# Turned tiles set between the quarters of the rising products, with attention's beginning and the merge's load order changed too

## The reference

```python
z  = x @ w_in                                   # queries, keys, values, indexer, gates
ya = sparse_attention(...)                      # 8 heads, top-256 keys by an indexer
yb = sliding_window_attention(...)              # 8 heads, window 128, sinks
merged = sigmoid(gA) * (ya @ w_pa) + sigmoid(gB) * (yb @ w_pb)
x1 = layer_norm(alpha * x + merged @ w_o, ln1_g, ln1_b)
u  = x1 @ w_up                                  # 1024 -> 6144
c  = conv_b + sum(shift(u, j) * conv_w[j] for j in range(3))   # causal, per channel
x2 = layer_norm(alpha * x1 + (gelu(c[:, :3072]) * c[:, 3072:]) @ w_down, ln2_g, ln2_b)
```

## Time and profile before

| | us |
|---|---|
| median of 3 runs | 3387.13 (3385.55 to 3394.36) |
| the profiled execution | 3393.38, of which the span 3391.6 |
| PE busy | 3236.4 (95%) |
| DVE busy | 2445.2 (72%) |
| ACT busy | 1673.5 (49%) |
| POOL busy | 1002.5 (30%) |
| mean granted TensorE clock | 0.981 of full speed |

### The profile page before, as it was taken

One profiled execution on the slowest core, in us unless ns is written; L12 is line 12 of the kernel. 1 busy time (PEld: TensorE's weight loads), 2 busy tenths in 40 slices (PEclk: granted clock), 3 DMA queues, 4 the chain that ended last, 5 costly groups with the idle time before them and its releaser, 6 DMA issues.

```text
span 3391.6 us, 40080 instructions
## 1 busy us (share of the span) xinstructions
PE 3236.4 (95%) x14200; PEld 2568.6 (76%) x14248; DVE 2445.2 (72%) x3632; ACT 1673.5 (49%) x2290; POOL 1002.5 (30%) x592
## 2 busy tenths in 40 slices
PE   7999999996899999989998999999999999999998
PEld 5788878874566666667887788887788888888887
DVE  5899999966666666446665799999888888343344
ACT  5669898215566676663222344444544444311211
POOL 1012232324566666650021134442233331000000
PEclk9999999997999999999999999999999999999999
DMA  6423333453232221035565332233222223533522
GB/s 173 60 75 100 97 109 100 130 167 97 74 84 64 59 65 49 7 111 194 177 248 174 113 104 102 100 122 132 97 91 75 94 87 133 193 109 112 174 98 95
DMA packets 219185, 376.78 MB, mean 111 GB/s; under 512 B 30573, under 2 KB 119933, under 8 KB 211182
## 3 DMA queue, kind: packets, MB, share of 16 engines
q1 hardware_dynamic: 217934, 369.86, 34.6%
q0 software_dynamic: 1056, 4.36, 0.3%
HBM read 276.24 MB, written 97.80 MB: 110 GB/s over the span
## 4 chain that ended last, share of the span: by engine, by line
PE 62%; DVE 6%; ACT 3%; issue 3%; DMA 2%; POOL 1%; SPq 1%; POOLq 0%; DVEq 0%; ACTq 0%
PE rs_ps L88 16%; PE rs_ps L89 15%; PE rs_ps L90 15%; PE rs_ps L2016 2%; PE rs_ps L2043 2%; PE rs_ps L2017 2%; PE rs_ps L1972 2%; PE rs_ps L2045 2%; PE rs_ps L2044 2%; PE rs_ps L2019 1%; PE rs_ps L2021 1%; PE rs_ps L2022 1%; DMA m_xp<-x 1%; DMA m_pr<-in_w_pb_dram 1%; DVE m_sg L1618 1%
## 5 line engine op out<-in xcount | busy, mean ns | idle before, releaser
L88 PE MATMUL rs_ps<-m_xh,m_uh 128*128 128x512 f32 x1344 | 526.8, 392 | 0.2 <-DVE m_ul L1666 0.2
L90 PE MATMUL rs_ps<-m_xh,m_ul 128*128 128x512 f32 x1344 | 524.8, 390 | 0.0
L89 PE MATMUL rs_ps<-m_xl,m_uh 128*128 128x512 f32 x1344 | 524.7, 390 | 0.0
L1160 POOL TENSOR_TENSOR plo<-pf,phi 128x1024 fp32r<-128x1024 f32 x168 | 401.7, 2393 | 266.5 <-ACT phi L1271 260.8
L88 PE MATMUL frt_acc<-frt_xh,frt_wh 128*128 128x512 f32 x864 | 338.8, 392 | 8.8 <-issue 4.5
L89 PE MATMUL frt_acc<-frt_xl,frt_wh 128*128 128x512 f32 x864 | 338.0, 391 | 0.0
L90 PE MATMUL frt_acc<-frt_xh,frt_wl 128*128 128x512 f32 x864 | 337.7, 391 | 0.0
L88 PE MATMUL rs_ps<-m_wh,m_hh 128*128 128x512 f32 x768 | 299.0, 389 | 1.4 <-DVE m_hl L1725 1.2
L90 PE MATMUL rs_ps<-m_wh,m_hl 128*128 128x512 f32 x768 | 298.8, 389 | 0.0
L89 PE MATMUL rs_ps<-m_wlo,m_hh 128*128 128x512 f32 x768 | 298.8, 389 | 0.0
L88 PEld LDWEIGHTS rs_ps<-m_xh,m_uh 128*128 128x128 f32 x1344 | 253.8, 189 | 52.9 <-DVE m_ul L1666 0.6
(11 more groups left out here) (289 smaller groups left out, 7429.7 us busy)
## 6 DMA issues: line engine op xcount, KB each, us to landing
m_ur<-in_w_up_dram SPq DMA_DIRECT2D x48, 1024.0 KB, 6.1
m_wr<-in_w_down_dram SPq DMA_DIRECT2D x60, 512.0 KB, 4.8
zt<-frt_out SPq DMA_DIRECT2D x108, 256.0 KB, 4.5
frt_wr<-in_w_main_dram SPq DMA_DIRECT2D x51, 512.0 KB, 4.1
ht<-m_cg SPq DMA_DIRECT2D x48, 512.0 KB, 3.4
...
```

The lines of the kernel that those rows point to most:

```text
L88: pe.matmul(out, ahi, bhi, start=first, stop=False)
L89: pe.matmul(out, ahi, blo, start=False, stop=False)
L90: return pe.matmul(out, alo, bhi, start=False, stop=last)
L1160: pool.tensor_tensor(plo[:, k % PS, :], pf[:, k % PS, :], f32(phi[:, k % PS, :]), ALU.subtract).then_inc(S["pl"], 1)
```

## The change

It has four parts.

1. SP's order in the merge: the gates of unit u + 2 are loaded in iteration u, behind the weights of unit u + 3, so each unit's gates go out one iteration later; the residual rows go from m = 2 to 5 to m = 4 to 7; the rows of operands 0 and 1 from m = 3 to m = 5 of the last quarter.
2. Attention's beginning: the first `blo` goes from POOL to DVE, and `round_near(1)` from behind the first exponential to right behind `round_values`.
3. PE at k = 0, 23 and 24: a product can be given an operand to turn, and then one tile follows each of its quarters (three passes). The product's counter is raised ahead of the fourth tile. The wait for all of `rd1` now stands ahead of product 0.
4. ACT's and DVE's orders at k = 23 and 24 follow this. Their order at k = 0 is unchanged.

```diff
@@ load_unit (SP)
+            def load_weights(u):
                 if u >= R:
                     sp.wait_ge(T["ab"], u - R + 1)
                 for a, w in enumerate((w_pa, w_pb)):
-                    sp.dma_start(pr[u % R][:, a], w[m]).then_inc(pld[u % R], 16)
+                    sp.dma_start(pr[u % R][:, a], w[u % KT]).then_inc(pld[u % R], 16)
+
+            def load_gates(u):
+                q, m = u // KT, u % KT
                 if u >= R:
                     sp.wait_ge(T["md"], u - R + 1)
...
                     if u + R < NU:
-                        load_unit(u + R)
+                        load_weights(u + R)
+                    if u and u + R <= NU:
+                        load_gates(u + R - 1)
...
-                    if q and 2 <= m < 2 + TB:
-                        sp.wait_ge(st[m - 2], 16 * q)
-                        load_res(TB * q + m - 2)
+                    if q and m >= TB:
+                        sp.wait_ge(st[m - TB], 16 * q)
+                        load_res(TB * q + m - TB)
...
-                    elif q == 3 and m == 3:
+                    elif q == 3 and m == 5:
                         load_rows(0, 0)
                         load_rows(0, 1)
@@ POOL
-            pool.wait_ge(S["bhd"], 1)
-            pool.tensor_tensor(blo[:, 0], near[:, 0], f32(bhi[:, 0]), ALU.subtract).then_inc(S["bl0"], 1)
@@ ACT
                     round_values()
+                    round_near(1)
...
                     exponential(first[b] + x)
-                    if b == 0:
-                        round_near(1)
@@ DVE, attention and k = 23, 24
             dve.tensor_copy(bq[:, 1, :, P:2 * P], nearq[:, 1, :, 0:P]).then_inc(S["rnd"], 1)
+            dve.wait_ge(S["bhd"], 1)
+            dve.tensor_tensor(blo[:, 0], near[:, 0], f32(bhi[:, 0]), ALU.subtract).then_inc(S["bl0"], 1)
...
-                if r != NS - 1:
-                    conv(r - 1, 0)
-                if r == NS:
-                    low_x(1, 5, 0)
+                conv(r - 1, 0)
                 if r < NK:
                     low(r, 6)
                 if r == NS - 1:
                     low_x(1, 0, 0)
-                    conv(r - 1, 0)
+                elif r == NS:
+                    low_x(1, 5, 0)
@@ PE
+            def turn_tile(p, r, b):
+                i, n = 7 * p + r, TB * (7 * p + r) + b
+                if b == 0:
+                    pe.wait_ge(T[f"rl{i % 2}"], 16 * (i // 2 + 1))
+                if n >= 3:
+                    pe.wait_ge(T["xld"], n - 2)
+                for j in range(4):
+                    last = pe.transpose(ps[:, turn_bank(n), j * P:(j + 1) * P], xw[:, i % 2, b, j * P:(j + 1) * P], ident[:])
+                last.then_inc(T["tr"], 1)
...
-            def product(k, j):
+            def product(k, j, turned=None):
...
-                last.then_inc(T["pm"], 1)
+                    if kk == 3:
+                        last.then_inc(T["pm"], 1)
+                    if turned:
+                        turn_tile(*turned, kk)
...
-            product(0, 0)
-            turn(0, 2, 0)
-            turn(0, 2, 1)
...
+            pe.wait_ge(T["rd1"], NB)
+            for j in range(5):
+                product(0, j, (0, j + 2))
             product(0, 5)
             for k in range(1, NK):
...
+                beside = {NS - 1: {1: (1, 0), 6: (1, 1), 3: (1, 2), 4: (1, 3), 5: (1, 4)}, NS: {0: (1, 5), 2: (1, 6)}}.get(k, {})
```

More of the change, by code:

```diff
@@ L1469, in _ @@
                 if r == NS - 1:
-                    high_x(1, 1, 1)
                     high_x(1, 2, 0)
@@ L1885, in _ @@
                 elif r == NS:
+                    low_x(1, 6, 0)
                     low_x(1, 6, 1)
@@ L1890, in _ @@
                     low_x(1, 2, 1)
-                    low_x(1, 3, 0)
                 if more:
@@ L1896, in _ @@
                 if r == NS - 1:
+                    low_x(1, 3, 0)
                     low_x(1, 3, 1)
[L1898 removed]
                 if more:
@@ L1901, in _ @@
                 if r == NS - 1:
+                    low_x(1, 4, 0)
                     low_x(1, 4, 1)
@@ L2075, in turn @@
                 for b in (2 * half, 2 * half + 1):
-                    n = TB * i + b
-                    if n >= 3:
-                        pe.wait_ge(T["xld"], n - 2)
-                    for j in range(4):
-                        last = pe.transpose(ps[:, turn_bank(n), j * P:(j + 1) * P], xw[:, i % 2, b, j * P:(j + 1) * P], ident[:])
-                    last.then_inc(T["tr"], 1)
+                    turn_tile(p, r, b)
+            def turn_tile(p, r, b):
[7 more added lines that the diff above has]
+                last.then_inc(T["tr"], 1)
             def products(u):
```

30 lines of the change are left out of this document (6 added, 24 removed).

## The result

The changed kernel takes 3409.95 us (median of four runs, 3407.98 to 3411.45) against 3386.34 (3380.3 to 3394.36) for the kernel before: the ratio is 1.0066, with a 95% interval of 1.0048 to 1.0085. It is 22 us slower, where +8 was forecast and 3408 was the upper end of the range. The direction came out. So did the waits worked out for attention, k = 0, and k = 23 and 24, within 2 us each; the merge did not, and the clock took more than was put down for it.

What follows compares the result with a forecast made beforehand. PE, busy for 95% of the span, was taken as the bound. Terms -8.0, -5.0, +9.4 and +3.2 gave -0.4, with the clock +8.0; on the median 3387.13 that made 3395.1 us, range 3374 to 3408.

Steps and rivals of the forecast that it cites:

- Attention, -8.0: Attention's beginning: first exponential 3.4 us earlier, and 4.6 of a 7.39 us DVE wait reaching PE; -8.0 us.
- The merge, -5.0: Merge: gains at the last unit and last quarter, less costs of later gates, sum to -5.0 us.
- The last unit's -6.6: Merge, last quarter: the last unit's stall goes, -4.8 us, and the slow stretch behind it, -1.8.
- The terms for the gates: Merge: later gates cost +1.6 us in the first quarter, +1.2 and +1.4 at second units of quarters 1 and 2.
- -2.6: Merge, last quarter's first stalls: later gates let rows go out some 3 us earlier, 2.6 of it gained.
- a sign of being wrong: Merge, quarter 0: the prediction is wrong if the gates make ACT wait for over 4 us.
- k = 0, +9.4: k = 0: stalls grow from 5.4 to 16.7 us; with 1.9 of slow stretch set aside, +9.4 us.
- k = 23 and 24, +3.2: k = 23 and 24: stalls +5.7 us, single tiles +0.8, slow stretches of 3.3 set aside; +3.2 us.
- The clock: Outside the merge, six stalls over 2.7 us each bring a slow stretch of PE's clock at 1.4 us: +8.4.
- The rival "slow clock": Places that change: eleven of thirteen stalls bring slow stretches at 1.6 us, +17.6 for 8.4, total 3404.3; chance 0.22.
- The third rival: k = 0, 23 and 24: tiles hide their chains, few stalls reach 2 us, total about 3371; chance 0.14.
- The Trainium skill's rule: Attention's beginning: shared SBUF interfaces would let POOL's memset hold DVE's moved two-input subtract, giving 1.7 us less.

Runs made afterwards that it cites:

- e5: The kernel before with only the rows of operands 0 and 1 loaded at m = 5 of the last quarter: 3386.16 us, ratio 0.9991.
- e2: The kernel before with SP's changed load order in the merge alone: 3395.51 us, ratio 1.0026.
- e13: The kernel before with the changed load order but without its later gates: 3385.12 us, ratio 0.9988.
- e6: The kernel before with only the gates loaded one unit later: 3402.08 us, ratio 1.0041.
- e15: The kernel before with only the first blo moved to DVE, round_near(1) left in place: 3385.73 us, ratio 0.9994.
- e7: The kernel before with k = 0's tiles between quarters, the rd1 wait, and ACT's and DVE's orders there made to fit: 3391.55 us, ratio 1.0007.

## Why the prediction was wrong, point by point

- **Attention, -8.0: right in its sum, by luck in its parts.** It measured -8.6 in the mean of the profiles, of which -7.2 are waits of PE and the rest clock. The parts were 3.4 and 4.6 and came out near 2 and 5. The first fell short because the cast ahead of the subtract took 2.37 us for 0.67; the second gave more than I let reach PE. The chain `phi`, `plo` was next, as said, but not as long as allowed for.
- **The merge, -5.0: this is the step that failed.** The last unit's -6.6 held: -6.0 between the mean of six profiles with e5's line and that of seven without. The terms for the gates were too small by far. They stood at +1.6, +1.2 and +1.4, with -2.6 for a gain of theirs in the last quarter, +1.6 in all; by e2 and e13 the gates cost 7.2 us, and in e6, without the other moves, 15. In the first quarter I priced the gates of one unit, where ACT waited for three, 4.6 us in sum, which is over the 4 us that I had named as a sign of being wrong. PE's waits there grew by 4.9 us (by 3.0 in e2) for +1.6. At the second units the wait became 3.10 and 2.75 where I had 2.1 to 2.3, with a slow stretch behind each that I had not counted there. The -2.6 did not come: the two waits of the last quarter fell by 1.05 in sum, and in e2 not at all. The chain that I named, from POOL's last difference to the quarter's first pass, is as said: 21.0 us lie between the starts of the two in the kernel before, the changed one, e2, e5, e13 and e15. The rows also went out earlier, at 1743.57 for a mix begun at 1747.57, before at 1744.91 for 1745.32. But they landed no earlier: POOL's first difference of them began 7.9 us behind the start of the mix, 7.5 before, and ahead of the last group POOL still stood for 7.89 us:

```profile
1782.97 1.29 POOL L1197 TENSOR_TENSOR m_xd<-m_xp 128x512 f32<-128x512 f32 x1 [7.89 <-DMA m_xp<-x]
```

  I had taken an earlier issue for an earlier landing. What held the rows up on the way is not shown.
- **k = 0, +9.4 with the clock apart: right.** Waits of 15.1 us for 16.7, each at its place; e7 shows that they are ACT's and DVE's orders, as argued.
- **k = 23 and 24, +3.2 with the clock apart: right in its waits,** all five within 0.4 us.
- **The clock: under-sized.** I removed 7.0 us of old slow stretches and added 8.4, net +1.4. The merge kept its losses, which takes back 1.8, and k = 0 and 23 together lost 7.3 more than before: +7.1. It shows little in the sum, because two errors met: at k = 0, 23 and 24 waits and tiles came out 2.3 us below what I had, and the clock 4.1 above. The rival "slow clock" had the mechanism, with a net of +10.6 for those 7.1, and its 3404.3 lacked the merge.
- **The base.** The sum of the stretches in the profiles is +17.0, on a pair of profiles 17.2 apart, where I had +8.0: of the 9.0 missing the merge is 9.3, attention 2.1 the other way, and the rest 1.8. The medians are 23.6 apart, the ratio of the runs gives 22. What lies between is the spread from run to run.
- **The third rival's 3371** is the median less 16 and leaves out the clock that it speaks of.
- **The Trainium skill's rule** ("GPSIMD Engine Reference", section 1 "Specifications") gave 1.7 us less for attention, by a two-input subtract held by the memset; I went by the row against it. No run shows that: the moved subtract took 2.27 us in each of the eight profiles that have it. About as much was lost all the same, by the cast ahead of it, which has one input and is drawn out in six of nine kernels without the moved subtract too. The same line of the page also names DVE instructions in a 2-port perf mode; whether the cast is one, no run here shows.
